# Third value unit of the input projection moved into the stream of the modulation weights

## The reference, cut to what matters

```python
m = silu(cond) @ w_ada + b_ada            # shift, scale, gate, twice: 6 x 2048
h = rmsnorm(x, n1g) * (1 + sc1) + sh1     # 640 x 2048
u = h @ w_in                              # GLU input | q | k | v | gate A | gate B
glu_in, q, k, v, ga, gb = split(u)        # v: 4 heads x 128 columns
...                                       # attention, convolution, gates, experts
```

## Time and profile before

| what | value |
|---|---|
| median of 3 runs | 3076.98 us (3076.11 to 3078.21) |
| profiled execution | 3075.98 us, span 3074.2 us |
| TensorE busy | 2965.9 us, 96% of the span |
| VectorE, ScalarE busy | 2162.5 us (70%), 1417.6 us (46%) |
| raw<-in_w_ada | 96 transfers of 1024 KB |

### The profile page before, as it was taken

The page is one execution under the profiler, slowest core; times in us unless marked ns, Lnnn a source line. Parts: engine busy times, 40 slices in busy tenths (PEclk is TensorE's granted clock), DMA queues, the critical chain, the costliest instruction groups (busy, mean ns, idle before and its releaser), DMA issues.

```text
span 3074.2 us, 50690 instructions
## 1 busy us (share of the span) xinstructions
PE 2965.9 (96%) x20093; PEld 2511.3 (82%) x20093; DVE 2162.5 (70%) x2408; ACT 1417.6 (46%) x1627; POOL 325.8 (11%) x448
## 2 busy tenths in 40 slices
PE   5999999989999999999999998799999999999997
PEld 4899999989999999999999998466666666666665
DVE  5778876556666666674244333799999999999997
ACT  3223333333333333333122222577777777777775
POOL 0011210111101111110011111000100000001000
PEclk9999999999999999999999999899999999999998
DMA  9544433554545454453345434999999999999995
GB/s 401 230 145 130 136 123 99 186 192 168 203 163 201 173 189 181 169 192 125 116 167 185 133 120 158 339 380 394 381 378 390 391 392 397 393 390 377 382 404 167
DMA packets 131269, 756.45 MB, mean 246 GB/s; under 512 B 17552, under 2 KB 27840, under 8 KB 56656
## 3 DMA queue, kind: packets, MB, share of 16 engines
q1 hardware_dynamic: 98832, 636.54, 53.9%
q0 software_dynamic: 32272, 117.53, 12.3%
HBM read 686.87 MB, written 60.58 MB: 243 GB/s over the span
## 4 chain that ended last, share of the span: by engine, by line
PE 87%; DMA 5%; DVE 5%; ACT 1%; issue 1%; POOL 0%; DVEq 0%; SPq 0%; POOLq 0%; ACTq 0%
PE pu L1158 23%; PE pu L1165 12%; PE pu L776 10%; PE pu L777 10%; PE pu L778 10%; PE pu L858 3%; PE pu L861 3%; PE pu L860 3%; PE pt L755 2%; PE pt L958 2%; DMA raw<-in_w_ada 2%; PE ps L861 2%; PE ps L860 2%; PE ps L858 2%; PE ps L936 1%
## 5 line engine op out<-in xcount | busy, mean ns | idle before, releaser
L2337 DVE TENSOR_TENSOR elo<-ering,ehi 128x2048 fp32r<-128x2048 f32 x384 | 871.7, 2287 | 92.5 <-ACT ehi L1559 88.4
L1559 ACT CAST ehi<-ering 128x2048 fp32r<-128x2048 f32 x384 | 731.4, 1912 | 242.3 <-PE pu L1165 242.2
L776 PE MATMUL pu<-hhi,whi 128*128 128x320 f32 x2144 | 679.8, 317 | 5.8 <-DVE hlo L2075 4.0
L778 PE MATMUL pu<-hhi,wlo 128*128 128x320 f32 x2144 | 663.9, 310 | 0.0
L777 PE MATMUL pu<-hlo,whi 128*128 128x320 f32 x2144 | 663.6, 310 | 0.0
L776 PEld LDWEIGHTS pu<-hhi,whi 128*128 128x128 f32 x2144 | 404.0, 188 | 15.0 <-issue 9.8
L777 PEld LDWEIGHTS pu<-hlo,whi 128*128 128x128 f32 x2144 | 404.1, 188 | 1.6
L778 PEld LDWEIGHTS pu<-hhi,wlo 128*128 128x128 f32 x2144 | 403.7, 188 | 0.0
L1158 PE MATMUL pu<-ehi,xhi 128*80 128x512 f32 x1024 | 320.7, 394 | 0.0
L1158 PE MATMUL pu<-ehi,xlo 128*80 128x512 f32 x1024 | 319.7, 393 | 0.0
L1165 PE MATMUL pu<-elo,xhi 128*80 128x512 f32 x1024 | 276.7, 392 | 0.0
(11 more groups left out here) (395 smaller groups left out, 4532.2 us busy)
## 6 DMA issues: line engine op xcount, KB each, us to landing
ering<-in_w_experts SPq DMA_DIRECT2D x384, 1024.0 KB, 9.3
raw<-in_w_ada SPq DMA_DIRECT2D x96, 1024.0 KB, 7.6
blocks<-in_w_in SPq DMA_DIRECT2D x72, 512.0 KB, 3.8
raw<-in_w_in SPq DMA_DIRECT2D x34, 1024.0 KB, 5.0
raw<-in_w_attn_out SPq DMA_DIRECT2D x16, 1024.0 KB, 5.4
raw<-in_w_out SPq DMA_DIRECT2D x16, 1024.0 KB, 4.9
gates_tanh<-th POOLq DMA_DIRECT2D x32, 320.0 KB, 2.4
gl<-gates_tanh POOLq DMA_DIRECT2D x32, 320.0 KB, 3.4
```

The source lines that it names most:

```text
L776: nc.tensor.matmul(o, whi[:, dk, w:w + 128], hi[:, kt, cols], start=kt == 0, stop=False)
L778: last = nc.tensor.matmul(o, wlo[:, dk, w:w + 128], hi[:, kt, cols], start=False, stop=kt == kts - 1)
L1559: nc.scalar.copy(ehi[:, j % AHEAD, :], ering[:, slot, :]).then_inc(ex_hi, 1)
L2337: nc.vector.tensor_tensor(elo[:, j % AHEAD, :], ering[:, slot, :], ehi[:, j % AHEAD, :].bitcast(F32), ALU.subtract).then_inc(ex_lo, 1)
```

## The change

The value unit 2 is loaded between unit 9 and unit 10 of the stream (`THIRD` = 10), so that units 10 to 31 use the next raw place each. ScalarE casts it to a place of its own (`w2hi`, over rows 0 to 3 of `xin`) behind its work for unit 9, VectorE makes `w2lo` (over the vectors t1 to t4) behind row 3 of `hlo`, and both give the raw place back. TensorE multiplies one row of it behind the row output of units 12, 14, ... 30, into the two banks of `ps`, and the last six rows behind the last rows of units 0 and 1, ahead of the turn of unit 0. Unit 3 takes the split places 0 and the banks of unit 1, in two halves, with the turn of unit 1 between them and that of unit 2 behind. The loads of `cos` and `sin` wait for unit 2's product and stand behind the first `store_v`. The copy-out of unit 2 reads `ps`.

```diff
@@ -38,6 +38,7 @@
 RAW, SPL = 4, 2
 A1, QN, GN, SN, TN, CN, ON = 2 * KT, 24, 16, 32, 16, 8, 16
 ADA = 6 * KT
+THIRD = 10
 U = 4
 US = 8
 G_Q = A1 - 2
@@ -71,7 +72,7 @@
 
 def ada_use(j):
 
-    return raw_use(j, 0, 1, 0, 0)
+    return raw_use(j + (j >= THIRD), 0, 1, 0, 0)
 
 
 def ada_of(j):
@@ -150,6 +151,8 @@
     rstd, o = at("rstd", [128, N], F32, o)
     nrm, _ = at("nrm", [128, 4, 8], F32, o - 2 * N * 4)
     assert o <= C0
+    w2hi, _ = at("w2hi", [128, UNIT], F32R, Y0)
+    w2lo, _ = at("w2lo", [128, UNIT], F32R, Y0 + KT * N * 4)
 
 
     zt, o = at("zt", [128, CT, ZW], F32, Y0)
@@ -365,6 +368,9 @@
 
     SEGS = [(0, 0, 0, HALF), (HALF, 1, 0, NL - HALF), (NL, 1, NL - HALF, HALF)]
 
+    THIRD_FROM = 11
+    THIRD_KTS = (A1 - THIRD_FROM) // 2
+
     def used_slot(n):
 
         return 16 if n < 4 else 16 * PAIRS if n < 8 else 0
@@ -437,9 +443,10 @@
         for d in range(2):
             sp.dma_start(wfirst[:, d, :], a["w_in"][d]).then_inc(first_loaded[d], 16)
         for j in range(A1):
+            if j == THIRD:
+                load(a["w_in"][2], *raw_use(THIRD, 0, 1, 0, 0))
             load(a["w_ada"][ada_of(j)], *ada_use(j), first=j < RAW)
-        for d in (2, 3):
-            load(a["w_in"][d], *raw_use(G_Q, 1, U, 0, d))
+        load(a["w_in"][3], *raw_use(G_Q, 1, U, 0, 3))
 
         def load_block(u, b, at_):
             d, h = NKV + 2 * u + b // 2, b % 2
@@ -533,9 +540,6 @@
         for dst, name in ((bada, "b_ada"), (norms, "norms"), (taps, "taps"), (convp, "convp"),
                           (sinks, "sinks")):
             pool.dma_start(dst[:], a[name]).then_inc(small_loaded, 16)
-        pool.wait_ge(h_lo, KT)
-        pool.dma_start(cost[:, :], a["cos"]).then_inc(tabs_loaded, 16)
-        pool.dma_start(sint[:, :], a["sin"]).then_inc(tabs_loaded, 16)
 
         def store_v(n):
             pool.wait_ge(v_read, n + 1)
@@ -560,6 +564,10 @@
 
         for n in range(NKV):
             store_v(n)
+            if n == 0:
+                pool.wait_ge(dense_mm, CREDIT + 3)
+                pool.dma_start(cost[:, :], a["cos"]).then_inc(tabs_loaded, 16)
+                pool.dma_start(sint[:, :], a["sin"]).then_inc(tabs_loaded, 16)
         for n, src in enumerate((hhi, hlo)):
             pool.dma_start(b12_d[n], src[:, 0:KH, HALF:N]).then_inc(kept, 16)
         for n in range(NKV):
@@ -818,6 +826,21 @@
             if kt >= LAG:
                 first_unit(1, kt - LAG)
 
+        def third_unit(k0, k1):
+            if k0 == 0:
+                pe.wait_ge(hi_ready, 3)
+                pe.wait_ge(lo_ready, 3)
+                pe.wait_ge(norm_t, 4)
+            for kt in range(k0, k1):
+                w = slice(128 * kt, 128 * kt + 128)
+                for c in range(2):
+                    o, cols = ps[:, c, 0:HALF], slice(c * HALF, c * HALF + HALF)
+                    nc.tensor.matmul(o, w2hi[:, w], hhi[:, kt, cols], start=kt == 0, stop=False)
+                    nc.tensor.matmul(o, w2hi[:, w], hlo[:, kt, cols], start=False, stop=False)
+                    last = nc.tensor.matmul(o, w2lo[:, w], hhi[:, kt, cols], start=False, stop=kt == KT - 1)
+            if k1 == KT:
+                last.then_inc(dense_mm, 1)
+
         rows = (row0, row1)
         for j in range(A1):
             kt, u = j // 2, j % 2
@@ -829,6 +852,8 @@
                 mean_over_channels(t2, ps, HALF, norm_mm)
             if j >= 5 and j % 2:
                 first_units((j - 5) // 2)
+            if j > THIRD_FROM and j % 2 == 0:
+                third_unit((j - THIRD_FROM) // 2, (j - THIRD_FROM) // 2 + 1)
         row_out(pt[:, (KT - 1) % 2, :], rows[(KT - 1) % 2][:, :], KT, 2)
         for kt in (KT - 2, KT - 1):
             first_units(kt)
@@ -844,11 +869,13 @@
                                            vst[:, 128 * t:128 * t + 128], ident[:, :])
             last.then_inc(v_tr, 1)
 
-        for d in range(1, NKV):
-            if d >= 2:
-                dense_start(d, d)
-                dense(d, d, d % 2, d % 2, hhi, hlo, 0, KT, 0, KT)
-            v_turn(d - 1)
+        third_unit(THIRD_KTS, KT)
+        v_turn(0)
+        dense_start(3, 3)
+        dense(3, 3, 0, 1, hhi, hlo, 0, KT // 2, 0, KT)
+        v_turn(1)
+        dense(3, 3, 0, 1, hhi, hlo, KT // 2, KT, 0, KT)
+        v_turn(2)
 
         def half_product(g, out, form, first):
 
@@ -867,7 +894,7 @@
                 g, p = 4 * u + n, b // 2
                 if n < 2:
                     if u == 0:
-                        pe.wait_ge(v_read, NKV - 1 + p)
+                        pe.wait_ge(v_read, NKV if p else 1)
                     else:
                         pe.wait_ge(rope_b, 2 * (u - 1) + p + 1)
                 pe.wait_ge(sp_hi, g + 1)
@@ -1205,10 +1232,10 @@
 
 
     def scalar_program(act):
-        def split_hi(slot, use, d, dk):
+        def split_hi(slot, use, d, dk, done=None):
 
             act.wait_ge(raw_loaded[slot], 16 * (use + 1))
-            act.wait_ge(dense_mm, d_done(d))
+            act.wait_ge(dense_mm, d_done(d) if done is None else done)
             nc.scalar.copy(whi[:, dk, :], raw[:, slot, :]).then_inc(hi_ready, 1)
             act.wait_ge(hi_ready, d + 1)
             act.sem_inc(raw_freed[slot], 1)
@@ -1250,6 +1277,13 @@
                 ada_read_out(*ada_use(j), pt[:, j // 2 % 2, :], rows[j // 2 % 2][:, :])
             if j >= 3 and j % 2:
                 modulated_hi((j - 3) // 2)
+            if j == THIRD - 1:
+                slot, use = raw_use(THIRD, 0, 1, 0, 0)
+                act.wait_ge(raw_loaded[slot], 16 * (use + 1))
+                act.wait_ge(h_lo, 4)
+                nc.scalar.copy(w2hi[:, :], raw[:, slot, :]).then_inc(hi_ready, 1)
+                act.wait_ge(hi_ready, 3)
+                act.sem_inc(raw_freed[slot], 1)
         modulated_hi(KT - 1)
 
         def ahead(i, k, body, first, stride, d0, count, nxt):
@@ -1268,7 +1302,7 @@
                 act.wait_ge(v_tr, d)
                 act.wait_ge(vx_stored, 16 * d)
             nc.scalar.copy(vst[:, :].rearrange("p (c n) -> p c n", c=2),
-                           pu[:, 2 * (d % 2):2 * (d % 2) + 2, 0:HALF]).then_inc(v_read, 1)
+                           ps[:, :, 0:HALF] if d == 2 else pu[:, 2 * (d % 2):2 * (d % 2) + 2, 0:HALF]).then_inc(v_read, 1)
             act.wait_ge(v_read, d + 1)
             act.sem_inc(psum_free[d % 2], 1)
 
@@ -1329,9 +1363,8 @@
             nc.scalar.activation(gsig[:, 0:HALF], banks(v)[0], ACT.Sigmoid)
             nc.scalar.activation(gsig[:, HALF:N], u2[:, :], ACT.Sigmoid).then_inc(glu_sig, 1)
 
-        split_hi(*raw_use(G_Q, 1, U, 0, 2), 2, 0)
+        split_hi(*raw_use(G_Q, 1, U, 0, 3), 3, 0, CREDIT + 1)
         v_out(0)
-        split_hi(*raw_use(G_Q, 1, U, 0, 3), 3, 1)
         act.sem_inc(hi_ready, SKIP)
         v_out(1)
         v_tokens(0)
@@ -1700,6 +1733,7 @@
         first_lo(0)
         vec.wait_ge(norm_mm, 2)
         link(nc.vector.tensor_copy(rstd[:, :].rearrange(c2, c=2), ps[:, :, 0:HALF]))
+        vec.sem_inc(norm_t, 1)
         first_lo(1)
         vec.wait_ge(small_loaded, 16 * 5)
         nc.vector.tensor_scalar(negsink[:, :], sinks[:, :], -1.0, None, ALU.mult)
@@ -1716,6 +1750,13 @@
             vec.wait_ge(h_hi, kt + 1)
             nc.vector.tensor_tensor(hlo[:, kt, :], xin[:, kt, :], hhi[:, kt, :].bitcast(F32),
                                     ALU.subtract).then_inc(h_lo, 1)
+            if kt == 3:
+                slot = THIRD % RAW
+                vec.wait_ge(hi_ready, 3)
+                nc.vector.tensor_tensor(w2lo[:, :], raw[:, slot, :], w2hi[:, :].bitcast(F32),
+                                        ALU.subtract).then_inc(lo_ready, 1)
+                vec.wait_ge(lo_ready, 3)
+                vec.sem_inc(raw_freed[slot], 1)
 
         def lower(g, src):
 
@@ -1846,8 +1887,7 @@
                 vec.wait_ge(zrow_stored[m % 2], 16 * (m // 2))
             nc.vector.tensor_tensor(zrow[:, m % 2, :], c2b[:, :], gsig[:, :], ALU.mult).then_inc(glu_z, 1)
 
-        split_lo(*raw_use(G_Q, 1, U, 0, 2), 2, 0)
-        split_lo(*raw_use(G_Q, 1, U, 0, 3), 3, 1)
+        split_lo(*raw_use(G_Q, 1, U, 0, 3), 3, 0)
         vec.sem_inc(lo_ready, SKIP)
         first_form(0)
         for k in range(KH):
```

## The result

The changed kernel takes 3081.76 us (median of 20 runs, 3079.56 to 3085.24) against 3077.64 us (20 runs, 3075.64 to 3082.07) for the kernel before in the same comparison. The ratio is 1.0012, with a 95% interval of 1.0007 to 1.0018: 0.12% or about 4 us slower, less than the 0.2% set as the bound of no change, but with an interval that leaves out 1. The span of the profiled execution is 3079.2 us against 3074.2.

The account below looks back on a forecast made before the run. DMA paced the stream, TensorE the stretch behind it. +5.2 for unit 31, -8.85 for matmuls, +1.1 for banks, +5.3 waiting for VectorE gave +2.8; 3075.98 + 2.8 + 1.0 gave 3079.8 us, range 3075.6 to 3083.0.

Parts of the forecast that it names:

- the bound of the stream: From unit 13 on, TensorE sets the pace: a pair of units takes 5.38 us against 4.97 for the transfers.
- Unit 31: Last w_ada unit of the stream, claimed to start at 109.8 us, 5.2 us later than before.
- the first turn: TensorE's first turn behind the stream, claimed at 127.1 us, where it came at 116.58 before.
- the wait for the banks: TensorE's unit 3 waits until ScalarE copies out unit 1's banks, claimed to add 1.1 us.
- VectorE's wait: Behind the stream, VectorE waits from 125.0 to 129.8 us for the first T1 cast: 4.8 us.
- the product at 149.23: TensorE's first block product, claimed to start at 149.1 us instead of 146.29, 2.8 us later.
- the forecast's own case: Total time of 3078.3 to 3081.5 us, given a chance of 0.62.
- all engines are 2.8 us late together: After VectorE catches up by about 170 us, the 2.8 us delay is carried unchanged to the end.
- about 3 us of cover: In the stream, the third unit's split ends near 55.7 us; its place's next transfer has its turn at 59.0.
- The gain survives: Rival: VectorE isn't held behind the stream, so the kernel is 2.5 us faster, 3074.5 us; chance 0.08.
- The gaps suffice: Rival: matmuls behind a row output overlap and the stream's 107.1 us holds; +0.1, 3077.1 us; chance 0.15.
- The clock rival: TensorE's 2.8 us hole between units 9 and 10 drops the clock; 2.8 us per pair; 0.08 for over 1.2 pairs.

Follow-up runs that it names:

- casts_first: The changed kernel with ScalarE's first three T1 casts moved ahead of the copy-out of unit 1, the fourth behind it; ratio 1.0003 to the kernel before.
- balanced: seven_and_one with ScalarE's order altered: one T1 cast ahead of unit 1's copy-out, one behind, six ahead of unit 2's; ratio 0.9989 to the kernel before.
- filled: The changed kernel with 8 unread matmuls of constants in TensorE's idle time ahead of the first product; ratio 1.0010 to the kernel before.
- none_in_stream: turn_first with all 16 rows of the third unit multiplied behind the stream, loading and splitting still in it; ratio 1.0020 to the kernel before.
- balanced_filled: balanced with 5 unread matmuls of constants between units 9 and 10 of w_ada; ratio 0.9988 to the kernel before.
- seven_and_one: turn_first with 7 rows of the third unit in the stream, one in the gap ahead of the last row, 8 behind; ratio 1.0004 to the kernel before.
- turn_first: The changed kernel with the turn of unit 0 ahead of the last six rows of the third unit on TensorE; ratio 1.0008 to the kernel before.

## Why the prediction was right

**Right, step by step.** TensorE became the bound of the stream behind unit 13, with a pair at 5.28 us (units 16 to 31, 70.67 to 109.95, are seven pairs and one unit of 2.32) instead of 5.38. Unit 31 came at 109.95, forecast 109.8; the first turn at 127.21, forecast 127.1; the wait for the banks 0.97, forecast 1.1; the first T1 cast at 129.40, forecast 129.3; VectorE's wait 4.63, forecast 4.8; the product at 149.23, forecast 149.1. That the copy-out of unit 1 holds the casts, these VectorE, and VectorE the product, was shown by casts_first and balanced: without the holds, the product starts 34.65 us behind unit 31 instead of 39.28.

**Mis-sized: 2.8 us, measured 4.8 at the later mark and about 4 in the median.** The measured 3081.76 lies in the range of 3075.6 to 3083.0, but 2.0 us above the forecast of 3079.8 and just outside the forecast's own case, 3078.3 to 3081.5. 0.7 of the 2.0 is the kernel before, whose median is 3077.64 in this comparison and was 3076.98 when I wrote. The step at fault is the sentence that from the product on "all engines are 2.8 us late together". I had priced the low clock only behind the hole in the stream and not behind the 5 us of idle time that my own sum put in front of the product. Its price is 1.8 us (8.89 less 7.12 in `filled`). 2.9 + 1.8 is 4.7, the later mark +4.8.

**Wrong in the working, without effect on the sum.** Two errors nearly cancel in unit 31, so that 109.95 met 109.8 was in part luck. The pairs were cheaper than I took (the nine from unit 13 to 31 took 47.73 us, 0.7 less than nine of 5.38). In return unit 13 started at 62.22 instead of 61.5. That lateness is older than the third unit: unit 9 already started at 49.18, where it was at 48.46 in the kernel before,

```profile
48.46 1.08 PE L755 MATMUL pt<-raw,condw 128*32 128x128 f32 x32 [1.06 <-DMA raw<-in_w_ada]
```

and from unit 9 to unit 13 the changed kernel takes 13.04 us, the 10.56 of the kernel before (one of its two pairs took 5.58) and one place of 2.48. I had also claimed about 3 us of cover for the raw place of the third unit. The rows of SyncE's issues say otherwise, two up to 52 us, the next at 56.47:

```profile
48.49 2.16 SPq L438 DMA_DIRECT2D raw<-in_w_ada  x2
...
56.47 2.07 SPq L438 DMA_DIRECT2D raw<-in_w_ada  x3
```

SyncE waits for VectorE to give back the place (w2lo runs from 54.09 for 2.29 us), only units 10 to 12 have been issued behind the third unit by then, and the transfers thin out to 330 GB/s from 56 to 60 us. Against 422 that is, as an estimate, (1 - 330/422) x 4, some 0.9 us of transfer time. All eight profiles with the third unit in the stream have a share of 0.86 to 0.96 between 54 and 58. What the gap costs at unit 31 isn't shown. From unit 9 to unit 31 the four kernels whose unit 31 waits for its transfer take, beyond the kernel before and one place of 2.48, 0.9 us (none_in_stream), 0.6 (balanced), 0.5 (balanced_filled) and nothing (seven_and_one), all with the same gap; the scatter of the stream is as large. No kernel with a place of its own for the third unit was run.

**The rivals.** "The gain survives" was false for the change as made, and it is what `balanced` reached (-3.9 us at the product) once the orders of TensorE and ScalarE and the number of rows in the stream were altered. "The gaps suffice" fell at unit 31. The clock rival was half right: a low clock followed the hole, as the Trainium skill ("TensorE: Matmul & The Clock Gate", section "HAM oscillation — how this bites in real kernels") says of bursts with DMA waits between them, and this trace agrees (0.57 at 54 to 58 us). It cost nothing that shows in the changed kernel's own profile, where unit 13 still waited 0.69 us for its transfer, and 0.3 to 0.9 us at unit 31 in the three other kernels with ten rows, less than the 2.8 us that I had set for a whole pair. It cost 1.8 us where I hadn't looked, ahead of the product.

## What to carry to other kernels

When work is taken from a full engine, follow each hand-written order of the other engines up to the next thing that engine needs: here one copy-out, waiting for a turn that had moved 10 us back, held casts, and through them a second engine, for more than the whole gain. If the sum then contains an idle time of TensorE, price the first matmuls behind it at half clock too. Moving work into gaps pays only as much as the gaps hold (0.65 us per pair here, against 1.07 of work); fewer rows in the stream, with a late one in a gap behind it, put unit 31 earlier than ten did (107.06 to 108.38 against 109.95 to 110.86).

## What the runs showed of the hardware

An idle time of TensorE of 2.0 to 3.6 us ahead of the product was followed by a granted clock of 0.57 to 0.63 over four microseconds in all four kernels that had it (2.05 us in casts_first, 3.55 in turn_first, 2.04 in none_in_stream, 2.06 in seven_and_one), although TensorE had worked without a break for over 14 us before, at full clock. In the kernel before, 1.59 us ahead of 111.22 was not followed by one. In single microseconds the clock is at 0.50, the 1.2 GHz level, and it may fall only when the matmuls already run again, as in seven_and_one, whose product starts at 144.01:

```profile
144.00:145.00 1.00, 0.99 (x7) 1.00 (x8) 0.93 (x3) 0.00 (x0) 0.96 (x2) 1.00 0.46 37
145.00:146.00 1.00, 1.00 (x6) 1.00 (x6) 0.96 (x3) 0.00 (x0) 0.00 (x0) 0.51 0.62 131
```

The product, 7.1 us at full clock, took 8.65 or 8.66 us in all four, whether the idle time was 2.04 or 3.55 us, and 8.89 behind 4.95. Read from these five products, the first two microseconds of idle time cost 1.5 us beyond themselves, and the next three 0.2 more.
